# q and k copied from PSUM unscaled by ScalarE, with eps times x's mean square added to the head norms in PSUM

## What is computed

```python
def rmsnorm(x, g):
    r = lax.rsqrt(jnp.mean(xf * xf, axis=-1, keepdims=True) + EPS)
    return (xf * r * g.astype(jnp.float32)).astype(x.dtype)

z = rmsnorm(x, p['attn_norm_g']) @ p['w_in']
q, k, v, u = split_projection(z)          # 1024, 256, 256, 1024 columns
q = rmsnorm(q, p['q_norm_g'])             # over each head's 64 features
k = rmsnorm(k, p['k_norm_g'])
attn = sliding window attention with sinks and ALiBi (window 128)
y_ssm, h_re, h_im = ssm_mixer(u, h0, ...) # complex diagonal scan, 64 groups of 16 channels
g = gelu(y_ssm); ssm_out = g * sigmoid(g @ w_glu + b_glu)
h = x + concat(rmsnorm(attn), rmsnorm(ssm_out)) @ w_out
y = h + relu(rmsnorm(h) @ w_mlp_up) ** 2 @ w_mlp_down      # D_FF = 8192
```

## Time and profile before

| | |
|---|---|
| median of 3 runs | 1255.66 us (1255.35 to 1256.86) |
| the profiled execution's own time | 1255.49 us |
| its span in the trace | 1253.4 us |
| TensorE busy | 1205.3 us, 96% |
| VectorE busy | 721.3 us, 58% |
| ScalarE busy | 412.1 us, 33% |
| GpSimd busy | 152.9 us, 12% |
| TensorE's mean granted clock | 0.983 |

### The profile page before, as it was taken

One profiled execution on the slowest core, in us unless ns is written; L12 is line 12 of the kernel. 1 busy time (PEld: TensorE's weight loads), 2 busy tenths in 40 slices (PEclk: granted clock), 3 DMA queues, 4 the chain that ended last, 5 costly groups with the idle time before them and its releaser, 6 DMA issues.

```text
span 1253.4 us, 20187 instructions
## 1 busy us (share of the span) xinstructions
PE 1205.3 (96%) x8478; PEld 1128.4 (90%) x8478; DVE 721.3 (58%) x718; ACT 412.1 (33%) x493; POOL 152.9 (12%) x92
## 2 busy tenths in 40 slices
PE   7999968898999998999999999999999999999997
PEld 5677646577999998999999999999999999999997
DVE  8678679674656554554445544455555544555443
ACT  5000012364445433333333333333333333333331
POOL 2331341000000000010001100010001100010001
PEclk9999998997999999999999999999999999999999
DMA  7333222235444544545554445545544454545552
GB/s 264 134 105 134 68 67 72 107 135 144 150 163 142 186 167 137 167 156 180 168 167 153 160 160 168 168 152 161 182 166 157 159 172 166 168 152 166 181 164 103
DMA packets 54329, 190.33 MB, mean 152 GB/s; under 512 B 7768, under 2 KB 9304, under 8 KB 53848
## 3 DMA queue, kind: packets, MB, share of 16 engines
q1 hardware_dynamic: 54248, 189.09, 45.5%
HBM read 185.82 MB, written 5.28 MB: 152 GB/s over the span
## 4 chain that ended last, share of the span: by engine, by line
PE 92%; DVE 3%; issue 2%; ACT 1%; POOL 0%; POOLq 0%; DMA 0%; ACTq 0%; DVEq 0%
PE psum L1220 92%; DVE states L822 1%; PE psum L1341 0%; DVE q_t L661 0%; DVE r_b L786 0%; DVE states L661 0%; DVE mov_b L1044 0%; ACT gate L549 0%; POOL states L1146 0%; POOL h_t L1146 0%; POOLq L115 0%; DVE w_lo L652 0%; ACT w_hi L419 0%; DMA small<-in_small 0%; ACT pt_head L532 0%
## 5 line engine op out<-in xcount | busy, mean ns | idle before, releaser
L652 DVE TENSOR_TENSOR w_lo<-w_raw,w_hi 128x1024 fp32r<-128x1024 f32 x288 | 401.8, 1405 | 420.8 <-ACT w_hi L419 420.2
L1220 PE MATMUL psum<-mov_b,w_hi 128*128 128x288 f32 x2560 | 511.4, 296 | 6.0 <-issue 4.1
L419 ACT ACTIVATE w_hi<-w_raw 128x1024 fp32r<-128x1024 f32 x288 | 302.7, 1058 | 504.5 <-PE psum L1220 504.5
L1220 PEld LDWEIGHTS psum<-mov_b,w_hi 128*128 128x128 f32 x2560 | 411.8, 189 | 6.9 <-issue 4.7
L1220 PE MATMUL psum<-mov_a,w_hi 128*128 128x288 f32 x2048 | 407.6, 295 | 3.2 <-DVE s_relu L1098 3.2
L1220 PE MATMUL psum<-mov_b,w_lo 128*128 128x288 f32 x1280 | 377.2, 295 | 0.0
L1220 PEld LDWEIGHTS psum<-mov_a,w_hi 128*128 128x128 f32 x2048 | 328.7, 189 | 3.7 <-DVE s_relu L1098 3.7
L1220 PE MATMUL psum<-mov_a,w_lo 128*128 128x288 f32 x1024 | 301.2, 294 | 0.0
L1220 PEld LDWEIGHTS psum<-mov_b,w_lo 128*128 128x128 f32 x1280 | 243.0, 190 | 0.0
L1220 PEld LDWEIGHTS psum<-mov_a,w_lo 128*128 128x128 f32 x1024 | 193.9, 189 | 0.0
L1220 PE MATMUL psum<-x_g,w_raw 128*128 128x288 f32 x640 | 167.9, 421 | 20.6 <-DVE q_t L661 13.3
(11 more groups left out here) (165 smaller groups left out, 514.8 us busy)
## 6 DMA issues: line engine op xcount, KB each, us to landing
w_raw<-in_w SPq DMA_DIRECT2D x336, 512.0 KB, 3.5
h_t<-in_x SPq DMA_DIRECT2D x4, 576.0 KB, 6.8
out_y<-h_t SPq DMA_DIRECT2D x4, 576.0 KB
b_w<-in_b SPq DMA_DIRECT2D x1, 1024.0 KB, 5.5
c_w<-in_c SPq DMA_DIRECT2D x1, 1024.0 KB, 7.9
k_cache<-in_kc SPq DMA_DIRECT2D x1, 1024.0 KB, 5.6
v_cache<-in_vc SPq DMA_DIRECT2D x1, 1024.0 KB, 5.7
out_kc<-in_kc SPq DMA_DIRECT2D x1, 992.0 KB
```

The lines of the kernel that those rows point to most:

```text
L419: nc.scalar.activation(hi3[:, n % SLOTS, :], raw3[:, n % SLOTS, :], ACT.Copy) \
L652: nc.vector.tensor_tensor(lo3[:, n % SLOTS, :], raw3[:, n % SLOTS, :], hi3[:, n % SLOTS, :].bitcast(F32), ALU.subtract) \
L1220: return nc.tensor.matmul(out, lhs_t, rhs, start=start, stop=stop)
```

## The change

ScalarE copies q and k out of PSUM as they are (`raw_out`), g_kv's unit has two readers, and VectorE's `project_out` is left only for u and, for g_kv, for v's two banks. k is squared straight from PSUM. The Ln of the head norms has no bias; in its place `head_means` adds, for each of its banks, a product of 32 rows of ones with 32 rows of eps_x, each bank with another group of 32 rows. eps_x is a new tile, written by ScalarE from the bank of rms_x ahead of the first root: EPS/32 times x's mean square, plus EPS^2/32. An unused tile goes. TensorE waits for g_kv's readers ahead of kv_aux.

```diff
-    [("rms_x", 1), ("g_u0", 4), ("bu0", 16), ("g_u1", 1), ("g_kv", 1), ("y0", 4), ("g_q0", 1), ("bu1", 16),
+    [("rms_x", 1), ("g_u0", 4), ("bu0", 16), ("g_u1", 1), ("g_kv", 2), ("y0", 4), ("g_q0", 1), ("bu1", 16),
...
-        ssq_s, _ = sb("ssq_s", TOK)
+        eps_x, _ = sb("eps_x", TOK)
...
+            unit_full(act, UNIT["rms_x"])
+
+            nc.scalar.activation(eps_x[:, :], banks(UNIT["rms_x"], 1)[:, 0, :], ACT.Copy,
+                                 scale=EPS / 32 / D_MODEL, bias=EPS * EPS / 32)
             root(r_b, UNIT["rms_x"], 1.0 / D_MODEL)
...
                 unit_full(act, unit)
-                nc.scalar.activation(dst, banks(unit, n), ACT.Ln, bias=eps).then_inc(evacuated[unit % 2], 1)
-
-            unit_read(act, UNIT["g_kv"])
-            nc.scalar.activation(sq3[:, 0:2, :], kv3[:, 0:2, :], ACT.Square).then_inc(squared, 1)
+                nc.scalar.activation(dst, banks(unit, n), ACT.Ln).then_inc(evacuated[unit % 2], 1)
+
+            def raw_out(name, dst):
+
+                unit_full(act, UNIT[name])
+                nc.scalar.activation(dst, banks(UNIT[name], dst.shape[1]), ACT.Copy) \
+                    .then_inc(evacuated[UNIT[name] % 2], 1)
+
+            unit_full(act, UNIT["g_kv"])
+            nc.scalar.activation(sq3[:, 0:2, :], banks(UNIT["g_kv"], 2), ACT.Square).then_inc(squared, 1)
+            raw_out("g_kv", kv3[:, 0:2, :])
...
+            raw_out("g_q0", q3[:, 0:4, :])
             unit_read(act, UNIT["g_q0"])
             act.wait_ge(k_ready, 1)
             nc.scalar.activation(sq3, q3[:, 0:4, :], ACT.Square).then_inc(squared, 1)
...
+            raw_out("g_q1", q3[:, 4:8, :])
             unit_read(act, UNIT["g_q1"])
...
-            def project_out(name, dst):
+            def project_out(name, dst, first=0):
 
                 u = UNIT[name]
                 unit_full(dve, u)
-                tt(dst, banks(u), over_tiles(r_b[:, :], OUTS), ALU.mult).then_inc(evacuated[u % 2], 1)
+                tt(dst, banks(u)[:, first:OUTS, :], over_tiles(r_b[:, :], OUTS - first), ALU.mult) \
+                    .then_inc(evacuated[u % 2], 1)
...
-            project_out("g_kv", kv3)
+            project_out("g_kv", kv3[:, 2:4, :], first=2)
...
-            project_out("g_q0", q3[:, 0:4, :])
...
-            project_out("g_q1", q3[:, 4:8, :])
...
                 for k in range(n):
-                    done = mm(banks(u)[:, k, :], head_mean, squares[:, k, :])
+                    mm(banks(u)[:, k, :], head_mean, squares[:, k, :], stop=False)
+                for k in range(n):
+                    rows = slice(32 * k, 32 * k + 32)
+                    done = mm(banks(u)[:, k, :], ones[rows, :], eps_x[rows, :], start=False)
                 return done
...
             pe.wait_ge(squared, 1)
+            unit_read(pe, UNIT["g_kv"])
             head_means("kv_aux", sq3, 2)
```

## The result

| | before | after |
|---|---|---|
| median of 5 runs | 1255.66 us (1254.05 to 1259.5) | 1265.29 us (1262.47 to 1269.84) |
| ratio after to before | | 1.0078, 95% interval 1.0049 to 1.0106 |
| the profiled execution's own time, its span | 1255.49, 1253.4 us | 1262.47, 1260.7 us |

The kernel is 9.6 us slower. The forecast was 1257.6, with 1254.0 to 1260.5 as its range.

The account below looks back on a forecast made before the run. TensorE, 92% of the chain that ended last, was taken as the bound. Root +1.79, VectorE's queue -1.24, qn0's eps products +0.80, clock +1.90, g_q1's end -1.10 gave +2.15 on 1255.49: 1257.6 us, range 1254.0 to 1260.5.

Parts of the forecast that it names:

- The first root: eps_x ahead of the root puts Sqrt's load on the path: +1.79 us; low clock behind unchanged, bounds -1.5 to +0.8.
- rivals D and E: First root: D, Sqrt's load stays early, 1256.4, chance 0.08; E, root pauses 1.28 us after its load, 1258.9, 0.04.
- k's norm and the eps products: At kv_aux: k's norm from PSUM worth nothing; each set of eps products 0.8 us, there hidden in the stall.
- rival B: At qn0 and qn1 the eps products do not overlap: 2.0 us a set, 1260.0 in all; chance 0.14.
- The two waits one behind the other: TensorE resumes at 185.3, not 191.26, but waits again before qn0 for ScalarE's Square; VectorE's queue gains 1.24 us.
- Rival A: Before qn0 the stall is really gone, as qn0 does not wait for the scan: -6.3 us, 1249.2; chance 0.05.
- The clock at qn0: After a stall of 6 to 9 us before qn0, TensorE runs at half clock: +1.9 us, bounds 0 and 2.4.
- Rival C: Clock does not fall before qn0, or its half-pace time lies under the stall: 1255.7; chance 0.12.
- The end of g_q1: From qn0 to glu0: qn0's eps products +0.8, low clock +1.9, q's second half copied by ScalarE -1.1 us.
- part 5: q's second half leaves on ScalarE: scores(0) -1.9, qn1's eps products +0.8, net -1.1 us, passed on from 243.00.
- part 2: k's norm from PSUM and kv_aux's eps products: worth nothing, 0.8 us a set, at kv_aux inside the stall.
- One low stretch more or fewer: Forecast's own spread: after some later short wait, about 3 us at clock 0.50, some 1.6 us each, 1256.0 to 1259.3.

Follow-up runs that it names:

- the six profiles: Profiles of six kernels with eps_x ahead of the root: 100.77, 99.07, 98.89, 98.66, 99.13 and 100.77 us for TensorE's stage behind the root.
- both repairs: Changed kernel with the root ahead of eps_x and eight small products more ahead of the loop: 1256.29 beside 1254.90, ratio 1.0002.
- x2_after_pad: Changed kernel with eight small products (32 instructions) more in the stall behind kv_aux, moving the loop's head: 1258.31 beside 1254.12, ratio 1.0031.
- x1_before_pad: Kernel before with ten small products and one wait (41 instructions) more in the stall behind kv_aux: 1261.72 beside 1254.12, ratio 1.0059.

## Why the prediction was wrong, point by point

**The first root: right in kind, the bounds failed.** The load for Sqrt stands behind eps_x as forecast, 1.28 us (eps_x took 0.41 instead of 0.50), the root at 43.59 starts 0.01 us behind the load's end, so rivals D and E are out, and TensorE's idle time grew by 1.7 where 1.79 was forecast. What failed is "I expect the same again and count nothing", with at most +0.8 for the low clock in the stage behind. It costs 1.2 to 3.3 us in the six profiles. At qn0 I had made the low clock grow with the stall, and here, where the stall grows by half, I had not. As a rule of proportion it does not hold either: in the changed kernel 4.8 us of idle time are followed by some 10 us of work at half clock here, and 6.4 us of it ahead of qn0 by less than 4.

**k's norm and the eps products: right.** A set costs 0.7 us at full clock where 0.8 was taken, so rival B, 2.0 for a set, does not hold by the trace.

**The two waits one behind the other: right.** TensorE was forecast to return at 185.3, to stand for 4.8 us, and again for 6 to 9 us before qn0; the root's stage had made the trace 3.7 us later than forecast by then (5.47 instead of 1.79), and less these it returned at 185.1, and stood for 4.49 and 6.39. Qn0's start moved by +4.37, which is the delay that reached the scan, 5.47, less 1.10 for q's scaling (1.24 forecast). Rival A is out for the order as it is, and was right about what could be had: A had 6.3 us under the kernel before, and with qn0 four tiles later and both repairs it is 7.1.

**The clock at qn0: right in size.** 1.9 us were taken, 2.2 measured by filling the wait. Rival C is out. The way to the 1.9, between two stalls by their length, has no support in the runs, so that it is so near is partly luck.

**The end of g_q1: right.** The sum from qn0 to glu0 was 0.8 + 1.9 - 1.1 = +1.6; it is +1.3.

So the early part's own cost, without the stage's clock, is close to the sum: x2_after_pad, which has everything but the loop's gaps, comes to glu0 3.6 us later than the kernel before, which is the forecast's +2.15 and the 1.4 us (98.89 instead of 97.48) by which the clock behind the root was undersized. Its median stands at +4.2, with 2.4 to 5.3 as the interval.

**The loop: not in the forecast at all.** No step and no rival held that TensorE's ten products and one wait more, all of them far ahead of it, could cost anything 500 us later. This is what put the time out of the range: 1.0078 beside x2's 1.0031, and 1.0059 for the 41 instructions alone. The step that failed is the end of part 5, "From 243.00 the chain is TensorE's own again, so the shift is passed on": the shift was not passed on as it was, but grew by 6.3 us from the first turn on, 2.3 us of it waits (6.4 beside 4.1) and 4.0 slower work. With it failed part 2, whose "At kv_aux this lies in the stall" costs the new instructions only where they run. The trace of before had the sign of it, two waits of about 2 us for "issue" at the loop's turns, on the chain; I did not ask what ended them.

**The spread.** "One low stretch more or fewer" was too little. The changed kernel's five runs lie over 7 us. At each turn of the changed kernel a wait in two parts, 3.4 and 3.0 us together, goes with work at half clock (0.50 over 738.50 to 742.00, and 0.53 over 948.50 to 952.00), where the kernel before has 0.50 over 735.90 to 739.00 and none at its second turn. In x1_before_pad's profile the loop takes 4.7 us more than before, 3.1 of waits and 1.6 of slower work; what else is in its median's 7.6 is not shown.

## What to carry to other kernels

When one early wait goes, look at the next wait of the same engine and at what ends it, and move the work between the two: here the copy on ScalarE gained nothing until qn0 was put four tiles later, and 7 us then (with both repairs). An activation put ahead of one with another function takes over its wait and leaves the table load behind it, on the path. Count an edit's instructions on an engine whose later loop is on the path, and read the waits at the loop's turn before and after; a few instructions of padding in a stall can be worth more than the edit.

## What was not expected of the hardware

- The cost of a loop's place: 64 instructions ahead of it cost 11 us (8.7 in the loop itself by the profile), 72 cost nothing measurable (1265.23 and 1255.24). The wait at a turn is 1.8 to 2.9 us in the kernels without a gap, and 4.9 to 5.9 us pass from its start until the second block's work when the head is close to the end of a block.
- TensorE's clock can cost more than the idle time ahead of it: 1.7 us more of idle time at the first root were followed by slow work that cost 1.2 to 3.3 us more, a different amount in profiles with the same idle time.
- Useless products in a wait made the kernel 3.5 us faster by the ratios (1.0031 to 1.0003), 2.2 us of it shown as clock.
- Four 32-row products of 288 columns, each in a row group and a bank of its own, take 0.7 us together between products of 128 rows.
